# A hybrid decoder layer with expert retrieval: the gather ring filled in another order, first dots and sums among tile 1's norm and the last projections, and the recurrence steps respread

## The reference, cut to what matters

```python
s1 = jnp.einsum('nhc,hkc->nhk', q[:, :, 0], k1)      # 128 keys each
s2 = jnp.einsum('nhc,hkc->nhk', q[:, :, 1], k2)
v1, i1 = lax.top_k(s1, 16);  v2, i2 = lax.top_k(s2, 16)
sc, pos = lax.top_k((v1[..., :, None] + v2[..., None, :]).reshape(n, 8, 256), 16)
e = i1[pos // 16] * 128 + i2[pos % 16];  g = jax.nn.softmax(sc, axis=-1)
hsel = jnp.einsum('tsd,td->ts', u_tab[e], x)          # dot with the gathered row
wgt = g * jax.nn.gelu(hsel, approximate=False)
out = jnp.einsum('ts,tsd->td', wgt, v_tab[e])         # weighted sum of gathered rows
```

## Time and profile before

| | |
|---|---|
| median of 3 runs | 1692.57 us (1689.67 to 1696.16) |
| profiled execution | 1692.44 us, span 1690.7 us |
| TensorE, VectorE busy | 1217.4 us (72%), 1249.3 us (74%) |
| ScalarE, GpSimd busy | 703.5 us (42%), 903.2 us (53%) |
| DMA | 605.43 MB, mean 358 GB/s |
| chain that ended last | DMA 39%, PE 24%, DVE 17%, POOL 6% |
| mean granted TensorE clock | 0.847 of full |

### The profile page before, as it was taken

One profiled execution on the slowest core, in us unless ns is written; L12 is line 12 of the kernel. 1 busy time (PEld: TensorE's weight loads), 2 busy tenths in 40 slices (PEclk: granted clock), 3 DMA queues, 4 the chain that ended last, 5 costly groups with the idle time before them and its releaser, 6 DMA issues.

```text
span 1690.7 us, 19411 instructions
## 1 busy us (share of the span) xinstructions
PE 1217.4 (72%) x5360; PEld 611.3 (36%) x5360; DVE 1249.3 (74%) x2965; ACT 703.5 (42%) x1990; POOL 903.2 (53%) x1135
## 2 busy tenths in 40 slices
PE   7998887666776777775987767675767666767555
PEld 5887755222333433332332323232323222323110
DVE  3878764888798878777778777677767677767775
ACT  3322223555444444434454654343434343434444
POOL 0365012567576655564466656566655555656662
PEclk9999999788789989887998877788777786878876
DMA  6321467999999999999899999999999999999996
GB/s 202 125 88 50 97 208 273 351 375 357 417 393 416 420 416 419 417 416 417 352 384 418 419 417 419 418 418 413 418 407 419 402 418 395 420 418 418 415 410 272
DMA packets 109308, 605.43 MB, mean 358 GB/s; under 512 B 22904, under 2 KB 25336, under 8 KB 42640
## 3 DMA queue, kind: packets, MB, share of 16 engines
q0 software_dynamic: 74880, 545.29, 79.1%
q1 hardware_dynamic: 34304, 58.89, 10.5%
q10 hardware_dynamic: 16, 0.02, 0.0%
HBM read 600.97 MB, written 3.19 MB: 357 GB/s over the span
## 4 chain that ended last, share of the span: by engine, by line
DMA 39%; PE 24%; DVE 17%; POOL 6%; issue 5%; ACT 4%; DVEq 4%; SPq 0%; POOLq 0%
DMA arena<-in_uv,arena 37%; PE ps L1018 10%; DVE arena L1928 9%; PE ps L591 5%; POOL arena L2164 4%; DVEq L1364 4%; DVE arena L1367 3%; PE ps L940 2%; POOL arena L2163 2%; PE ps L663 2%; DVE arena L1373 1%; ACT arena L1326 1%; ACT arena L1322 1%; PE ps L635 1%; DVE arena L1370 1%
## 5 line engine op out<-in xcount | busy, mean ns | idle before, releaser
L1018 PE MATMUL ps<-arena 128*64 128x512 f32 x2048 | 659.0, 778 | 388.2 <-ACT arena L1326 387.4
L1928 DVE CUSTOM_DVE_ANT_0 arena<-arena 128x1024 f32<-128x1024 f32 x520 | 637.7, 1228 | 285.7 <-DMA arena<-in_uv,arena 262.6
L2164 POOL DMA_INDIRECT arena<-in_uv,arena x520 | 616.8, 1186 | 90.2 <-POOL arena L2163 9.3
L2163 POOL TENSOR_TENSOR arena<-arena 1x1 f32<-1x1 f32 x520 | 204.2, 393 | 530.8 <-PE ps L1018 430.4
L1018 PEld LDWEIGHTS ps<-arena 128*64 128x64 f32 x2048 | 151.3, 164 | 772.1 <-ACT arena L1326 533.8
L1320 ACT ACTIVATE arena<-arena 128x1 f32<-128x1 f32 x520 | 106.0, 204 | 730.2 <-DVE arena L1928 724.7
L1326 ACT ACTIVATE arena<-arena 128x64 f32<-128x64 f32 (+1 forms) x520 | 182.7, 351 | 16.9
L1322 ACT ACTIVATE arena<-arena 128x1 f32<-128x1 f32 x520 | 154.5, 297 | 17.0
L1367 DVE TENSOR_TENSOR arena<-arena 64x8 uint32<-64x8 f32 (+8 forms) x312 | 134.7, 433 | 23.8 <-ACT arena L1067 15.3
L591 PE MATMUL ps<-arena 128*128 128x264 f32 (+1 forms) x608 | 140.6, 385 | 4.5 <-DVE arena L1367 3.3
L940 PEld LDWEIGHTS ps<-arena 128*128 128x128 f32 x1024 | 122.1, 198 | 36.0 <-issue 35.9
(11 more groups left out here) (176 smaller groups left out, 949.3 us busy)
## 6 DMA issues: line engine op xcount, KB each, us to landing
arena<-in_win SPq DMA_DIRECT2D x38, 512.0 KB, 3.4
arena<-in_wqk SPq DMA_DIRECT2D x60, 256.0 KB
arena<-in_wout SPq DMA_DIRECT2D x24, 512.0 KB, 5.0
arena<-in_uv,arena POOLq DMA_INDIRECT x520
arena<-in_xp SPq DMA_DIRECT2D x4, 512.0 KB, 6.9
out_yp<-arena SPq DMA_DIRECT2D x4, 512.0 KB
arena<-in_wqk SPq DMA_DIRECT2D x15, 128.0 KB
arena<-in_const SPq DMA_DIRECT2D x1, 864.0 KB, 8.0
```

Source lines behind the costliest of these rows:

```text
L1018: last = mm(ps[64 * q:64 * q + 64, b + c, :], diag[:, (s + q) % 8, :], ring[:, (s + q) % RING, D + 512 * c:D + 512 * c + 512], start=(s == ...
L1928: v.tensor_tensor_reduce(out=ring[:, s % RING, 0:D], in0=ring[:, s % RING, 0:D], in1=row, scale=1.0, scalar=0.0, op0=MUL, op1=ADD, accum_o ...
L2163: pool.tensor_tensor(carrier[:, 1:2], carrier[:, 0:1], carrier[:, 0:1], ALU.add).then_inc(S["carried"], 1)
L2164: pool.indirect_dma_start(out=ring[:, s % RING, :], out_offset=None, in_=a["uv"][:, :], in_offset=bass.IndirectOffsetOnAxis(ap=idx[:, t, s ...
```

## The change

- **The ring.** The slot of a gather is no longer k mod 8 but comes from a table. Gathers 0 to 4 go to slots 0 to 4, gathers 5 to 8 again to slots 0 to 3 once gathers 0 to 3 have been used, and 9 to 11 to the fresh slots 5 to 7. The wait for all 38 copies moves from gather 5 to gather 9. From gather 12 on each slot comes from the gather eight before.
- **The opening.** Dots 0 to 3 stand among tile 1's norm and feature copies, their weighing among ScalarE's copies, and their sums between the last projections, whose results go to PSUM banks 5 and 6 from the 36th on. `choose` for unit 1 stands in one piece behind dot 4, its gate behind dot 7. Sigmoid and swish of the convolution group move behind weighing 5 and dot 8.
- **Choosing.** From unit 2 on ScalarE copies the scores out of PSUM. Unit 2's steps start two gathers later, its query at slot 6 of unit 0 and its scores at slot 11.
- **The steps.** `pace` has three slopes: 0 to 22 over gathers 10 to 70, to 121 over gathers 70 to 186, then three steps in five gathers.
- **Weights.** The three blocks kept aside are issued together. The eight blocks of the second projection go at `slot_used` 148, 151, 154 (once the recurrence's `p2` is copied) and 171, 173, ... 179.
- **The start.** The features of tile 4 stand ahead of the means of tiles 2 and 3.

```diff
-    return 2 * (k - START) // 3
+    if k <= E_END:
+        return C_TOK * (k - START) // (E_END - START)
+    if k <= OUT_AT:
+        return C_TOK + (C_OUT - C_TOK) * (k - E_END) // (OUT_AT - E_END)
+    return C_OUT + 3 * (k - OUT_AT) // 5
-START = 8
-W_SLOT = 166
+START, E_END, OUT_AT = 10, 70, 186
+W_SLOTS = (148, 151, 154, 171, 173, 175, 177, 179)
+SLOT_OF = [0, 1, 2, 3, 4, 0, 1, 2, 3] + [(5, 6, 7, 4, 0, 1, 2, 3)[k % 8] for k in range(8 * 65)]
+FREE = (0, 1, 2, 3, 4, 9, 10, 11)
+FRESH = 9
...
+def z_bank(j):
+
+    return j % 2 if j < Z_HIGH else 5 + j % 2
...
-                elif 5 <= k < 5 + len(ASIDE):
-                    if k == 5:
-                        sp_.wait_ge(S["short_done"], 2)
-                    sp_.dma_start(w_aside[k - 5], a["wout"][:, OUT_ORDER[ASIDE[k - 5]], :]).then_inc(d_aside, 16)
+                elif k == 5:
+                    sp_.wait_ge(S["short_done"], 2)
+                    for i, j in enumerate(ASIDE):
+                        sp_.dma_start(w_aside[i], a["wout"][:, OUT_ORDER[j], :]).then_inc(d_aside, 16)
...
             features(1)
+            features(TILES)
             for t in XORDER[3:]:
                 mean(t, "sq_done", XPLACE[t] + 1, "mean_done")
-            features(TILES)
...
             first_out(1, 1, 8)
-            zcol(len(ZORDER) - zn[0] - 1)
+            zcol(3)
             turned(1, 0)
             turned(1, 1)
-            zcol()
             query(1)
             score(1)
+            pe.wait_ge(S["z_copied"], Z_HIGH)
+            sums(0, 0)
+            zcol()
+            sums(0, 2)
+            zcol()
...
-                    elif k == 5:
+                    elif k == FRESH:
                         pool.wait_ge(S["z_copied"], len(ZORDER))
-                    if k >= RING:
-                        pool.wait_ge(S["slot_used"], k - RING + 1)
+                    if k not in FREE:
+                        pool.wait_ge(S["slot_used"], LAST_IN[k] + 1)
...
+                    if k == 4:
+                        for step in range(STEPS - 1):
+                            choose(1, step)
+                    elif k == 7:
+                        choose(1, STEPS - 1)
+                    elif k == 8:
+                        conf_swish(1)
...
+            def score_copy(v):
+                act.wait_ge(S["score_mm"], v + 1)
+                act.wait_ge(S["idx_ready"], v)
+                f(scores, ps[:, 4, 256:512], ACT.Copy).then_inc(S["score_used"], 1)
...
             second_norm(1)
+            dve.wait_ge(S["xpair_done"], 1)
+            dot(0, 0)
             second_features(1, 0)
             second_features(1, 1)
-            conf_swish(1)
+            dot(0, 1)
+            dot(0, 2)
+            dot(0, 3)
```

162 lines of the change are left out of this document (94 added, 68 removed).

## The result

The changed kernel takes 1671.03 us (median of four runs, 1670.68 to 1674.85), the kernel before 1694.37 in the same session (four runs, 1689.67 to 1699.61). The ratio is 0.986, 95% interval 0.984 to 0.988: 23.3 us faster. Predicted were 1667 us and 25.6 us less, with a range of 1655 to 1684.

The account below looks back on a forecast made before the run. The end was taken as fixed by the first gather's start, the bytes behind it and DMA time below 417 GB/s. Terms -2.6 - 11.0 - 11.5 + 1.5 - 2.0 = -25.6 us from 1692.4 gave 1667 us, range 1655 to 1684.

Parts of the forecast that it names:

- part 1: Start: tile 4's features moved earlier let TensorE start 3.0 us earlier; 2.6 us gained, bounds 0 and 3.0.
- part 2: From tile 1's output projection to gather 16: earlier sums and gathers; 11 us gained, bounds 5 and 15.
- part 3: Gathers 16 to 79: respread mixer steps let VectorE catch up; 11.5 us gained, bounds 4 and 15.
- part 4: Gathers 70 to 186: the chain's steps 28% denser on VectorE; 1.5 us lost, range nothing to 5.
- part 5: Output projection of tiles 2 and 3: its six pieces and weight blocks moved; 2 us gained, bounds 0 and 6.
- A: Opening gained, but VectorE, 5 us late at gather 16, starves the ring on to gather 80; 1681 us, chance 19%.
- B: Nearly everything returned from start, opening, spread and projection pieces, ring full from gather 5; 39 us gained, 1653 us, chance 8%.
- C: A load decides the start and gather 12 or 16 comes after the queue runs dry; 1687 us, chance 9%.
- D: Gathers 70 to 186: the denser chain makes VectorE the bound, 38 us lost; slower at 1703 us, chance 6%.
- The rule that was to speak for D: VectorE reading two SBUF inputs shuts GpSimd out of their shared port, delaying descriptors; 0.2 us more per gather.

Follow-up runs that it names:

- Part 1 alone: The kernel before with only tile 4's features moved ahead of the means of tiles 2 and 3; 1693.1 us, ratio 0.999 to the kernel before.
- kept busy: The changed kernel with 33 small unread matmuls put where TensorE waits, around the transposes and ahead of the queries of tiles 0 and 1; 1673.6 us.
- four edits: The changed kernel with TensorE two gathers ahead, halved projection pieces, the key norm one step later and 33 small matmuls filling TensorE's waits; 1670.3 us.
- key norm later: The changed kernel with the second band's key norm one step later, which is two to three gathers; 1669.2 us, ratio 0.986 to the kernel before.
- lead of one: The changed kernel with TensorE one gather ahead of the other engines in the second band's steps instead of three; 1701.7 us, ratio 1.004 to the kernel before.
- the spread alone: The kernel before with the new pace and second-projection weights in two parts, without the new opening and start; 1686.5 us, ratio 0.996.
- old pace: The changed kernel with the second band's steps again at two steps in three gathers from gather 8 on, weights as changed; 1681.6 us, ratio 0.993.
- lead of two: The changed kernel with TensorE two gathers ahead of the other engines in the second band's steps instead of three; 1667.9 us, ratio 0.984 to the kernel before.

## Why the prediction was right, and where its terms were off

The reading that carried it held: the end is fixed by the first gather, the bytes, and the time below the full rate. Five terms gave 25.6 us; the profiled executions differ by 21.1. That the total came within 4.5 us is in part luck: parts 1, 2 and 4 were 7.7 us too hopeful, and 3.2 us came back in parts 3 and 5 and the rest. Single terms also rest on one execution each, and most of these places scatter by 2 to 4 us between programs (part 1 by 3.3).

| term | forecast | measured | off by |
|---|---|---|---|
| part 1, start | -2.6 | -1.1 | 1.5 |
| part 2, opening | -11.0 | -8.2 | 2.8 |
| part 3, spread | -11.5 | -12.4 | -0.9 |
| part 4, denser chain | +1.5 | +4.9 | 3.4 |
| part 5, projection | -2.0 | -3.3 | -1.3 |
| all else | 0 | -1.0 | -1.0 |

**Part 1.** The forecast put the first projection near 13.1 and it came at 12.89; the shift step came 0.65 us earlier, and the fourth projection 2.65. "Up to the first gather I see no other outside clock, so all of it shifts" is the sentence that failed. There was one: TensorE's granted clock. The lead was still 2.74 us when tile 0's query started and 1.1 when the first gather was issued, because that query took 1.62 us more. Part 1 alone shows no gain in the median, and over the twelve programs that have it the first gather was issued at 258.6 in the mean, as before, so even the 1.1 us may be chance.

**Part 2.** The moves came out step by step. The old times, less the 1.1 us gained by then, put the norm's end at 268.4; it ended at 267.19 + 1.29 = 268.48. The sums of slots 0 and 1 were to end at 278.9 and ended at 280.6; gather 9 was to go at 288.6 and went at 290.6. Some 1.5 of these 2 us are the second query: I took the row of 4.00 us, and it took 5.47 at the lower level. Kept busy, TensorE did it in 3.74. But that does not make up the 2.8 us by which the term was off. Where this query ran at the higher level gathers 0 to 15 still lost 7.3 us (kept busy), 7.1 (four edits), 6.5 (key norm later) and 6.4 (lead of one), against 7.8 here and 5.0 forecast. What holds the other 1.4 us or more stays open. The lump of choosing behind dot 4 and the softmax (3.02 us of waiting, forecast 5) cost no bandwidth; nothing was lost in gathers 8 to 15, as said.

On changes of table, the opening gives one more row, answering to the earlier trace rows:

```profile
298.08 1.28 ACT L1316 ACT_TABLE_LOAD   x1
...
299.37 0.31 ACT L1316 ACTIVATE arena<-arena 128x16 f32<-128x16 f32 x1
```

298.08 + 1.28 = 299.36: no pause. The drain that the Trainium skill, "ScalarE: Activation LUTs", What ACT_TABLE_LOAD costs, adds to each change is not there in this trace, and VectorE's wait for the softmax was 3.02 us, under the 5 forecast without a drain.

**Part 3.** Forecast 11.5, measured 12.4 between the two kernels and 10.8 and 11.5 in the two pairs that differ in the spread. What is left sits at gathers 32 to 47 (3.6 us).

**Part 4.** Its size was off: +4.9 at the upper bound of 5. VectorE came out at 84% (108.83 of 129 us) for a forecast of 83. At the old pace on the changed kernel 80 to 143 lost nothing, so the denser chain makes this loss. But busy time was the wrong thing to look at. TensorE's lead is counted in gathers, and the same three gathers hold more steps at the denser pace, so TensorE stops inside the chain with ready sums queued behind. A lead of two left 2.0 us of it (1.1 and 4.1 in the two other kernels that have it, the 4.1 not at 128 to 143 but before), against 2.7 to 5.3 with a lead of three. So the lead is shown to make the loss of 128 to 143; the slow dot is a part of 96 to 111. What makes up the rest was not settled.

**Part 5.** -3.3 measured. In the other kernels with the new pace and whole pieces gathers 192 to 223 lost 2.2 to 6.3 us against 9.6, and 10.5 with the lead of one. That is mostly more than the 2 us I took off, but this place scatters most, and which of the moved pieces and blocks did it was not tested.

**The rivals.** A (the debt moves) is refuted by the changed kernel itself, which lost 3.8 us in 16 to 79, and by the spread alone. B wanted 3.0, 15, 15 and 6 us of parts 1, 2, 3 and 5, and they gave 1.1, 8.2, 12.4 and 3.3. C fell with the opening: gathers 12 and 16 were issued at 297.1 and 308.1, before the packets of gathers 11 and 15 had ended (303 and 313). D did not come either: 505 to 780 lost 0.017 us per us, where D needed 0.09. The lead of one ended at 1701.7 us, next to D's 1703, but by another mechanism: there VectorE is not the bound, it waits 34.1 us for TensorE. The rule that was to speak for D shows in the trace and cost nothing: in the changed kernel the issue of a gather took 1.32 us in the mean where a dot ran beside it and 0.99 where none did, but from 484 to 780 us the mean issue was 1.15 us, against 1.18 before. The chances had an error of their own. Forecast, B and two thirds of A are 0.58 + 0.08 + 0.13 = 0.79, not 0.85.

## What to carry to other kernels

Read the time as bytes at the full rate plus the time lost below it, stretch by stretch; then a change that is spread over a program becomes a few terms that can each be checked. When a second stream of work is made denser, look at who runs ahead of whom, counted in steps and not in iterations, and at what is queued behind the engine that gets ahead. Do not book a gain of 1 to 3 us far ahead of the bottleneck when TensorE has idle gaps between: slow stretches of its clock, which cost 1.4 to 1.6 us each, come and go between there and the end.
